# Three layer norms handed on in single chunks, and four banks no longer cleared by products of zeros

## The reference

```python
def layer_norm(x, g, b):
    mu = jnp.mean(xf, axis=-1, keepdims=True)
    var = jnp.mean(jnp.square(xf - mu), axis=-1, keepdims=True)
    return (xf - mu) * lax.rsqrt(var + EPS) * g + b

x = layer_norm(ALPHA * x + g1 * attention(...), ln_g[0, 0], ln_b[0, 0])   # norm 0
h = modulate(x, sh2, sc2)                          # h * (1 + scale) + shift
x = layer_norm(ALPHA * x + g2 * (square(relu(h @ w1)) @ w2), ...)         # norm 1
h = modulate(x, sh1, sc1)                          # block 2: convolution mixer
x = layer_norm(ALPHA * x + g1 * conv_mixer(h, ...), ...)                  # norm 2
x = layer_norm(ALPHA * x + g2 * mlp(modulate(x, sh2, sc2)), ...)          # norm 3, output
```

## Time and profile before

| | |
|---|---|
| median of 3 runs | 1884.2 us (1884.07 to 1884.54) |
| the profiled execution's own time | 1888.57 us |
| its span, first to last instruction | 1886.7 us |
| mean granted TensorE clock | 0.972 of full |
| PE busy | 1764.3 us, 94% |
| DVE, ACT, POOL busy | 64%, 49%, 5% |
| DMA | 167 GB/s mean |

### The profile page before, as it was taken

How to read it: one execution, slowest core, us unless ns; L and a number is a source line. 1 busy time by engine, 2 the same in 40 slices (tenths; PEclk the granted TensorE clock), 3 DMA queues, 4 the chain that set the end, 5 groups by cost and what they waited for, 6 DMA issues and landing times.

```text
span 1886.7 us, 38215 instructions
## 1 busy us (share of the span) xinstructions
PE 1764.3 (94%) x13782; PEld 1648.5 (87%) x13782; DVE 1210.5 (64%) x2363; ACT 932.5 (49%) x1754; POOL 100.2 (5%) x101
## 2 busy tenths in 40 slices
PE   6989899999999888999999997988999989889997
PEld 5945899999999755899999997867799979879996
DVE  4545558888854599665555655477666665766665
ACT  4523455555554688455555553346444434434442
POOL 0000000000000265000000000000100010010000
PEclk8979999999999999999999998999999999999999
DMA  6535445555555678455655563301255545435551
GB/s 255 166 125 185 135 150 179 178 178 183 180 180 179 217 285 284 157 184 179 209 180 180 187 217 114 112 23 45 97 184 182 184 156 174 151 101 181 185 180 66
DMA packets 86500, 315.26 MB, mean 167 GB/s; under 512 B 9617, under 2 KB 9761, under 8 KB 86049
## 3 DMA queue, kind: packets, MB, share of 16 engines
q1 hardware_dynamic: 84816, 308.84, 49.6%
q10 hardware_dynamic: 1472, 4.47, 0.7%
q0 software_dynamic: 144, 1.05, 0.2%
HBM read 313.27 MB, written 1.05 MB: 167 GB/s over the span
## 4 chain that ended last, share of the span: by engine, by line
PE 88%; DVE 5%; issue 3%; ACT 2%; DMA 1%; ACTq 0%; DVEq 0%; SPq 0%
PE bank L487 15%; PE bank L488 15%; PE bank L489 15%; PE acc L487 11%; PE acc L488 10%; PE acc L489 10%; PE bank L785 4%; PE acc L546 2%; PE bank L567 2%; ACT arena L1017 1%; DMA route<-in_ada_w 1%; DVE small L1833 1%; PE acc L792 1%; PE bank L575 0%; DVE arena L1937 0%
## 5 line engine op out<-in xcount | busy, mean ns | idle before, releaser
L1413 DVE TENSOR_TENSOR w_lo<-raw,w_hi 128x512 fp32r<-128x512 f32 x982 | 653.0, 689 | 468.0 <-ACT w_hi L1017 467.2
L1017 ACT ACTIVATE w_hi<-raw 128x512 fp32r<-128x512 f32 x982 | 593.4, 627 | 423.6 <-PE acc L487 267.6
L487 PE MATMUL bank<-x_hi,w_hi 128*128 128x256 f32 x2224 | 639.3, 287 | 42.1 <-issue 20.3
L488 PE MATMUL bank<-x_lo,w_hi 128*128 128x256 f32 x2224 | 635.8, 286 | 0.0
L489 PE MATMUL bank<-x_hi,w_lo 128*128 128x256 f32 x2224 | 635.6, 286 | 0.0
L487 PEld LDWEIGHTS bank<-x_hi,w_hi 128*128 128x128 f32 x2224 | 433.5, 195 | 47.4 <-issue 29.3
L488 PEld LDWEIGHTS bank<-x_lo,w_hi 128*128 128x128 f32 x2224 | 433.6, 195 | 0.5 <-issue 0.5
L489 PEld LDWEIGHTS bank<-x_hi,w_lo 128*128 128x128 f32 x2224 | 433.2, 195 | 0.0
L487 PE MATMUL acc<-x_hi,w_hi 128*128 128x256 f32 x1024 | 290.7, 284 | 0.0
L488 PE MATMUL acc<-x_lo,w_hi 128*128 128x256 f32 x1024 | 290.3, 283 | 0.0
L489 PE MATMUL acc<-x_hi,w_lo 128*128 128x256 f32 x1024 | 290.3, 283 | 0.0
(11 more groups left out here) (238 smaller groups left out, 1828.0 us busy)
## 6 DMA issues: line engine op xcount, KB each, us to landing
raw<-in_peer_u SPq DMA_DIRECT2D x128, 512.0 KB, 3.5
raw<-in_peer_v SPq DMA_DIRECT2D x128, 512.0 KB, 3.5
raw<-in_mlp_w SPq DMA_DIRECT2D x128, 512.0 KB, 3.5
ada_x<-in_ada_w SPq DMA_DIRECT2D x64, 512.0 KB, 4.2
route<-in_ada_w SPq DMA_DIRECT2D x32, 512.0 KB, 4.5
raw<-in_w_in SPq DMA_DIRECT2D x25, 512.0 KB, 4.0
raw<-in_conv_w_in SPq DMA_DIRECT2D x24, 512.0 KB, 3.9
raw<-in_attn_w_in SPq DMA_DIRECT2D x18, 512.0 KB, 3.5
```

The costliest lines, as they stand in the source:

```text
L487: first = mm(dst, a[0], b[0], start=start, stop=False, **kw)
L488: mm(dst, a[0], b[1], start=False, stop=False, **kw)
L1017: return nc.scalar.activation(dst, src, f, **kw)
L1413: v.tensor_tensor(w_lo[:, unit(n, half)], raw[:, a:a + HALF], w_hi[:, unit(n, half)].bitcast(F32), ALU.subtract).then_inc(s["lo_done"], 1)
```

## The change

- `layer_norm(0..2)`: DVE no longer multiplies `res` by `ln_std`. For each chunk it forms `xm = res * factor * ln_std` (t), ACT forms `x_hi = xm + shift` rounded, and DVE forms `x_lo = (xm + shift) - x_hi`; t of chunk c+1 is issued before lo of chunk c. Semaphores `ln_t`, `ln_hi` and `ln_lo` count chunks.
- `project_chunks`: PE takes the first two weight tiles together, chunk by chunk, each chunk as soon as its lo is there. `unit_started` for the second tile is raised only in the last chunk.
- `hi_second` and an added `lo`: the second tile is split in front of the squares (ACT) and of the reciprocal (DVE).
- POOL multiplies `res` by `ln_std` itself (four operations of 128x512), after the last t, and then writes the next `x` as before. It writes no chunk of `xm`.
- `adaln` on DVE moves behind the chunks.
- `zero_acc` is gone. The first round of `v` and of both MLPs is written out ahead of the loop, and its first products carry the start flag. The wait for the ada columns moves in front of the first accumulating tile.
- In the first round of an MLP (`mlp_first`), ACT and DVE have no tile to split at q = 1 and split tile 3 (the third) at q = 0.

```diff
+            def project_chunks(name, dsts, starts, n):
+                for c in range(KC):
+                    if c % 4 == 0:
+                        w = [split_unit(name, q, c // 4) for q in range(2)]
+                    pe.wait_ge(s["ln_lo"], KC * n + c + 1)
+                    mms = [products(dsts[q], [part[:, c % 4 * P:(c % 4 + 1) * P] for part in w[q]], chunk(x_split, c),
+                                    c == 0 and starts[q], c == KC - 1, skip_group_check=True) for q in range(2)]
+                    if c % 4 == 0:
+                        mms[0][0].then_inc(s["unit_started"], 1)
+                for m in range(2):
+                    mms[1][m].then_inc(s["unit_started"], 1)
+                return mms[0][2], mms[1][2]
...
-            def zero_acc():
-
-                for b in range(4):
-                    mm(acc[b][:, :], C("zeros"), con[:, 0:512], start=True, stop=False, skip_group_check=True)
-
-            def accumulate(name, q, x, i):
+            def accumulate(name, q, x, i, first_tile=False):
...
-                                            [part[:, m * P:(m + 1) * P] for part in w], x, False, False,
+                                            [part[:, m * P:(m + 1) * P] for part in w], x, first_tile and c % 2 == 0, False,
...
             pe.wait_ge(s["ada_cols_ready"], 2)
-            zero_acc()
-            with pe.Fori(0, TILE["v"][1] // ROUND) as i:
+            for q in range(ROUND):
+                pe.wait_ge(s["gated_lo"], q + 1)
+                last = accumulate("v", q, chunk(x_split, q % 4), 0, q == 0)
+            last.then_inc(s["v_full"], 1)
+            with pe.Fori(1, TILE["v"][1] // ROUND) as i:
...
             def mlp(n):
+                name, hid = f"mlp{n}", f"hid{n}"
+                dsts = [opened(hid, q)[:, 0:T] for q in range(2)]
+                for q, last in enumerate(project_chunks(name, dsts, (True, True), 2 * n)):
+                    last.then_inc(full(hid, q), 1)
+                for q in range(2, 4):
+                    project(name, q, opened(hid, q)[:, 0:T], x_split).then_inc(full(hid, q), 1)
                 pe.wait_ge(s["ada_cols_ready"], 2 + n + 1)
-                zero_acc()
...
+            def hi_second(name, previous_done):
+
+                n = TILE[name][0] + 1
+                act.wait_ge(raw_full[n % RAW], 16 * (n // RAW + 1))
+                act.wait_ge(s["unit_started"], 2 * n + 2 - UNITS)
+                for half in range(2):
+                    if half:
+                        previous_done()
+                    a = n % RAW * D + half * HALF
+                    fn(w_hi[:, unit(n, half)], raw[:, a:a + HALF], ACT.Copy).then_inc(s["hi_done"], 1)
...
+                    for c in range(KC):
+                        act.wait_ge(s["ln_t"], KC * n + c + 1)
+                        fn(x_hi[:, c * T:(c + 1) * T], xm[:, c * T:(c + 1) * T], ACT.Identity, bias=ln_factor(ln_m, n, c)[1])\
+                            .then_inc(s["ln_hi"], 1)
+
+            def mlp_first(n):
+                for q in range(ROUND):
+                    if q != 1:
+                        hi_next(f"mlp{n}", max(q, 1))
+                    if q < 4:
+                        wait_full(act, f"hid{n}", q)
+                        fn(relu[:, q * T:(q + 1) * T], B(f"hid{n}", q)[:, 0:T], ACT.Relu).then_inc(free(f"hid{n}", q), 1)
...
             for n in range(3):
-                pool.wait_ge(s["ln_scaled"], 4 * n + 4)
-                for c in LN_POOL:
-                    last = nc.gpsimd.tensor_scalar(xm[:, c * T:(c + 1) * T], res[:, c * T:(c + 1) * T],
-                                                   *ln_factor(ln_m, n, c), ALU.mult, ALU.add)
-                last.then_inc(s["xm_pool"], 1)
+                pool.wait_ge(s["ln_t"], KC * (n + 1))
+                for k in range(4):
+                    pair = res[:, 2 * k * T:2 * (k + 1) * T].rearrange("p (c t) -> p c t", c=2)
+                    nc.gpsimd.tensor_tensor(pair, pair, ln_std.unsqueeze(1).to_broadcast([P, 2, T]), ALU.mult)\
+                        .then_inc(s["res_scaled"], 1)
+                pool.wait_ge(s["res_scaled"], 4 * (n + 1))
...
+                if n < 3:
+                    lo(TILE[("mlp0", "conv_u", "mlp1")[n]][0] + 1)
                 wait_freed(dve, f"var{n}")
                 then_wait(v.reciprocal(ln_std, ln_std))
...
+                for c in range(KC + 1):
+                    if c < KC:
+                        v.scalar_tensor_tensor(xm[:, c * T:(c + 1) * T], res3d[:, c, :], ln_factor(ln_m, n, c)[0], ln_std,
+                                               ALU.mult, ALU.mult).then_inc(s["ln_t"], 1)
+                    if c:
+                        a = slice((c - 1) * T, c * T)
+                        dve.wait_ge(s["ln_hi"], KC * n + c)
+                        v.scalar_tensor_tensor(x_lo[:, a], xm[:, a], ln_factor(ln_m, n, c - 1)[1], x_hi[:, a].bitcast(F32),
+                                               ALU.add, ALU.subtract).then_inc(s["ln_lo"], 1)
+                if n < ADA_2:
+                    adaln(2 + n, acc[1])
```

More of the change, by code:

```diff
@@ L483, in split_unit, with products @@
                 return w_hi[:, unit(n, half)], w_lo[:, unit(n, half)]
+            def products(dst, a, b, start, stop, **kw):
+                return (mm(dst, a[0], b[0], start=start, stop=False, **kw), mm(dst, a[0], b[1], start=False, stop=False, **kw),
+                        mm(dst, a[1], b[0], start=False, stop=stop, **kw))
             def three(dst, a, b, start, stop, **kw):
-                first = mm(dst, a[0], b[0], start=start, stop=False, **kw)
-                mm(dst, a[0], b[1], start=False, stop=False, **kw)
-                return first, mm(dst, a[1], b[0], start=False, stop=stop, **kw)
+                return products(dst, a, b, start, stop, **kw)[::2]
             def chunk(x, c):
@@ L979, in mlp @@
             def mlp(n):
-                pe.wait_ge(s["ada_cols_ready"], 2 + n + 1)
-                zero_acc()
-                name = f"mlp{n}"
-                with pe.Fori(0, TILE[name][1] // ROUND) as i:
+                name, hid = f"mlp{n}", f"hid{n}"
[4 more added lines that the diff above has]
+                    project(name, q, opened(hid, q)[:, 0:T], x_split).then_inc(full(hid, q), 1)
+                pe.wait_ge(s["ada_cols_ready"], 2 + n + 1)
+                for q in range(4):
+                    pe.wait_ge(s["hid_ready"], 32 * n + q + 1)
+                    last = accumulate(name, 4 + q, chunk((hid_hi, hid_lo), q), 0, q == 0)
+                last.then_inc(s["mlp_full"], 1)
+                with pe.Fori(1, TILE[name][1] // ROUND) as i:
                     for q in range(4):
-                        ps = opened(f"hid{n}", q, i)
-                        project(name, q, ps[:, 0:T], x_split, i, None if q else f"m{n}").then_inc(full(f"hid{n}", q), 1)
+                        ps = opened(hid, q, i)
+                        project(name, q, ps[:, 0:T], x_split, i).then_inc(full(hid, q), 1)
                     for q in range(4):
@@ L994, in _ @@
             layer_norm(1)
-            project_two("conv_u", "conv_u", x_split, "conv_in")
+            ps = opened("conv_u")
+            project_chunks("conv_u", [ps[:, 0:T], ps[:, T:2 * T]], (True, False), 1)[1].then_inc(full("conv_u"), 1)
+            for k in range(1, TILE["conv_u"][1] // 2):
+                project_pair("conv_u", k, "conv_u", k, x_split)
             project_two("conv_gate", "conv_gate", x_split)
@@ L1335, in _ @@
             layer_norm(0)
-            with act.Fori(0, TILE["mlp0"][1] // ROUND) as i:
+            mlp_first(0)
+            with act.Fori(1, TILE["mlp0"][1] // ROUND) as i:
                 mlp_round(0, i)
@@ L1353, in _ @@
             layer_norm(2)
-            with act.Fori(0, TILE["mlp1"][1] // ROUND - 1) as i:
+            mlp_first(1)
+            with act.Fori(1, TILE["mlp1"][1] // ROUND - 1) as i:
                 mlp_round(1, i)
@@ L1935, in layer_norm @@
                     wait_centered(dve, n, k)
-                    pair = res3d[:, 2 * k:2 * k + 2, :]
-                    v.tensor_tensor(pair, pair, over(ln_std, 2), ALU.mult).then_inc(s["ln_scaled"], 1)
-                if n < ADA_2:
-                    adaln(2 + n, acc[1])
-                dve.wait_ge(s["ln_scaled"], 4 * n + 4)
                 if n == 3:
+                    for k in range(4):
+                        pair = res3d[:, 2 * k:2 * k + 2, :]
+                        v.tensor_tensor(pair, pair, over(ln_std, 2), ALU.mult).then_inc(s["ln_scaled"], 1)
+                    dve.wait_ge(s["ln_scaled"], 4)
                     for c in range(KC):
@@ L1947, in layer_norm, with squared, mlp_first @@
                     return
-                for c in range(KC):
-                    if c not in LN_POOL:
-                        last = v.tensor_scalar(xm[:, c * T:(c + 1) * T], res3d[:, c, :], *ln_factor(ln_m, n, c),
-                                               ALU.mult, ALU.add)
-                    if c % 4 == 3:
```

(21 more changed lines are left out.)

40 lines of the change are left out of this document (18 added, 22 removed).

## The result

The changed kernel takes 1880.66 us (median of 20 runs, 1876.62 to 1882.37). The kernel before, run beside it, takes 1885.85 (20 runs, 1880.53 to 1892.0; the three shown ahead of the prediction are among them). The ratio is 0.9971, 95% interval 0.9964 to 0.9979: 5.5 us faster (5.2 by the medians). The forecast was 11.8, so less than half of it came, and 1880.66 lies outside the range of 1865 to 1877.5. The profiled execution took 1882.37.

A forecast was written before the change was run, and what follows sets the result against it. TensorE, busy 94% of the span, was taken as the bound. Gains of 2.1 at v and 2.1, 4.7 and 2.9 in norms 0 to 2 gave 11.8 us, from 1884.2 to 1872.4, range 1865 to 1877.5.

The forecast's parts named there:

- First products at R+1.7: Layer norms 0 to 2: first weight product at R+1.6, R being the end of the reciprocal; before, R+7.1 to R+8.8.
- lo every 0.80: Layer norms' chunk pipeline: VectorE starts an operation every 0.40, so one x_lo each 0.80 us, the last at R+7.0.
- the second tile: Layer norms: splitting the second weight tile ahead of time costs zero, hidden by VectorE's 3.25 us idle before the reciprocal.
- the loop entries: Three loops entered behind straight code: under 0.1 us each, taken as zero; rival of 3.5 each, 1883, chance 0.04.
- both stalls ahead of tile 4: First round of both MLPs: PE idle 1.4 to 3.7 us before tile 4, released by VectorE's weight subtraction.
- zero products at `v`: -2.1: Start of v: without zero products PE starts at 766.6 in place of 768.73, 2.1 us gained, later chunks moving along.
- clock: First two weight tiles of each norm: low clock after idle PE, so they end at R+9.2, not R+7.8.
- sum of norms 0 and 2: Gains forecast: norm 0 15.0-9.2-3.7 = 2.1 us, norm 2 15.8-9.2-3.7 = 2.9 us.
- the low clock takes more: Rival, norms 0 and 2: a second low stretch after the tile 4 stall, 1.9 to 2.9 each; 1877, chance 0.09.
- GpSimd: 1.04 each, 2.3 in norms 0 and 2, 0.8 in norm 1: Four GpSimd multiplies of 1.04 us hold VectorE's two-input operations, costing 2.3 more in norms 0 and 2, 0.8 in norm 1.
- The starting values: Kernel before, end of two weight tiles, read from one trace: R+15.0, R+14.7 and R+15.8 in norms 0, 1, 2.
- The upper rival: Rival, norms 0 to 2: all twelve GpSimd operations, 8.7 us, hold VectorE; 8.9 us slower, 1893, chance 0.04.

The follow-up runs named there:

- the change again: The changed kernel run once more with no edit, for a second trace: 1880.37 us, ratio 0.9971 to the kernel before.
- GpSimd late: Changed kernel, but GpSimd's four multiplies and eight x chunks wait until the first round's fourth squared chunk (convolution: conv_u_ready 4): 1873.74 us, ratio 0.9942.
- one-input: Changed kernel, but GpSimd's four residual multiplies become multiply-adds with one SBUF input, computing the residual wrongly: 1873.7 us, ratio 0.9938.
- the fastest kernel: Changed kernel with residual multiplies on VectorE, first-round weights of MLP tiles split earlier, and products of zeros at v and norms 1 and 2: 1864.17 us, ratio 0.9893.

## Why the prediction was wrong

*Right.* First products at R+1.7, lo every 0.80 (0.79 measured), two tiles at R+9.0 to R+9.4, no cost of the second tile or the loop entries (from the first accumulating product to the next round's first copy 14.60 before, 14.59 after), both stalls ahead of tile 4 released by DVE's weight subtraction, and GpSimd holding DVE.

*The step "zero products at `v`: -2.1".* PE started 2.1 earlier, and I carried that on: "the later chunks move along". The clock did not. The zero products had been work without use and also what kept PE busy over the gap. In six of the nine traces without them and without a filling, 1.4 of a possible 2.4 is given back, and 1.0 is left. The skipped question was the one asked of the norms: what did PE do before, and what does it now?

*The "clock" and the sum of norms 0 and 2.* I charged the low clock once, behind R+1.6, and forecast a stall of up to 3.7 ahead of tile 4 without charging it again. The rival "the low clock takes more" says just that; it got a chance of 0.09. It was the largest term missing from the sum: 1.5 to 1.7 in each MLP, 3.4 together in the trace of the change. It came in all three traces that had the stall of 2.6 ahead of tile 4 unfilled, and was gone when zeros filled it. The earlier trace rows had shown a slow first pair of tiles behind idle PE, so a forecast that writes down a long stall has to write down what follows it.

*The step "GpSimd: 1.04 each, 2.3 in norms 0 and 2, 0.8 in norm 1".* The mechanism was right, the size was not. A multiply takes 1.57 beside DVE, for 1.04 alone, and four hold DVE for their whole 6.3. The stops of tiles 3 and 4 together were 3.0 to 3.4, near the 3.7 forecast, since the longer hold also fell into gaps of DVE's own. Norm 1 lost 1.5 for 0.8. But what is bought by taking the hold away is far more than the 5.4 that I priced for the three norms. Between the traces of the change again and of GpSimd late it is 10.7 at their copies, of which 2.3 is lost again later, so 8.4; the whole kernels differ by 5.5 to 7 us (GpSimd late; one-input). The low stretches go with the hold. The upper rival, twelve operations holding DVE, is ruled out by the one-input run.

*The starting values.* The prediction took R+15.0 for norm 0 from one trace. At the high clock the same zero products end 3 us sooner and norm 0 is 1.9 earlier. That and the 1.4 of an untouched stage are draws of the clock. Other untouched code differs by more: the fourteen traces reach `v` at 762.7 to 767.5 and take 35.6 to 36.9 in the second half of the convolution. Such draws can account for the medians' 5.2 against the 7.4 of the edited places, but this is argued: three traces of the old norms do not tell how often each draw comes.

## What to carry to other kernels

Before work that looks useless is taken from TensorE, or a wait is accepted ahead of it, ask what it does in the time that is freed: an idle gap was paid twice here, once as itself and once as products at half the clock behind it. Do not hand GpSimd a two-input operation where VectorE is the feeder of TensorE; VectorE did the same four in 0.69 each, GpSimd took 1.57 and held VectorE all the while. And a reordering of a backlogged engine that frees only the next wait is worth nothing: with the hold and without it, the fourth tile's weights first gained at most 0.2 us by the next round. With the hold gone and the tiles behind moved as well, PE waited for no weights at all, 1.2 us less in each MLP. And before a stage's time is taken as a starting value, look at it in more than one trace.

## What was not expected

- A GpSimd multiply of 128x512 with two inputs stretches VectorE's two-input operations beside it from 0.42 to 0.69 up to 1.3 to 1.8, and itself from 1.04 to 1.57. With one input and numbers per partition it lasts 1.20, and the weight subtractions beside it 0.67 to 1.09.
- A gap of 1.40 us ahead of `v`, behind narrow products, was enough for some 15 products at 1.2 GHz in six of nine traces and not in three. Gaps of 1.3 to 1.6 ahead of tile 4 were followed by none (six, in three traces), gaps of 2.6 by one each time.
- Products of zeros are worth their place: 2.7 us of them inside a stall of 2.6 made it no longer and gave 1.3 to 1.5 back. Seven in all are part of the fastest kernel. The kernel before had twelve, which the change set out to remove.
